# Attention logits in paired banks, one mask matmul per bank, and the last two gate projections exchanged

## The reference

```
h  = rmsnorm(x) * g
z  = h @ w_in                  # columns: QA KA VA | QI KI WI | GA | QB KB VB GB
# group A: 8 heads of 64. The indexer scores sum_h w[t,h] * relu(qi.ki) keep the top 64 keys
#          of each query (chunk-causal, chunks of 64); softmax attention over the kept keys
# group B: 4 heads, two maps each (8 maps of 64): softmax(Q1K1) - lam * softmax(Q2K2), times V,
#          headwise rmsnorm, chunk-causal mask
y  = concat(oa * silu(ga), ob * silu(gb)) @ w_out
x  = x + rmsnorm(y)
e  = (p @ w_ple_proj) * sigmoid(x @ w_ple_gate)
x  = x + rmsnorm(e)
```

## Time and profile before

| | |
|---|---|
| median of 3 runs | 405.52 us (404.76 to 406.02) |
| span of the profiled execution | 403.8 us |
| PE busy | 389.4 us, 96% |
| DVE busy | 261.8 us, 65% |
| ACT busy | 225.3 us, 56% |
| mean granted TensorE clock | 0.998 of 2.4 GHz |

### The profile page before, as it was taken

How to read it: one execution, slowest core, us unless ns; L and a number is a source line. 1 busy time by engine, 2 the same in 40 slices (tenths; PEclk the granted TensorE clock), 3 DMA queues, 4 the chain that set the end, 5 groups by cost and what they waited for, 6 DMA issues and landing times.

```text
span 403.8 us, 5700 instructions
## 1 busy us (share of the span) xinstructions
PE 389.4 (96%) x1972; PEld 315.5 (78%) x1972; DVE 261.8 (65%) x450; ACT 225.3 (56%) x451; POOL 66.3 (16%) x122
## 2 busy tenths in 40 slices
PE   7798999999999999999999999999999999999993
PEld 6696777778777888888889878677877788888882
DVE  2837686659954458668686558765995445866733
ACT  4828545665755564544684545556575556454412
POOL 1515322031500000003005411203150000000000
PEclk9999999999999999999999999999999999999999
DMA  7999626334544237467655851733464413753002
GB/s 264 310 220 348 211 58 203 106 105 138 175 117 145 73 104 241 159 211 153 196 173 164 249 152 53 209 104 104 129 185 114 148 61 107 249 146 117 0 11 93
DMA packets 32075, 61.64 MB, mean 153 GB/s; under 512 B 2384, under 2 KB 4688, under 8 KB 32048
## 3 DMA queue, kind: packets, MB, share of 16 engines
q1 hardware_dynamic: 30928, 58.01, 46.0%
q0 software_dynamic: 1120, 3.28, 4.1%
HBM read 60.23 MB, written 1.05 MB: 152 GB/s over the span
## 4 chain that ended last, share of the span: by engine, by line
PE 79%; DMA 5%; DVE 5%; ACT 3%; issue 3%; POOL 3%; SPq 1%; DVEq 0%; POOLq 0%; ACTq 0%
PE proj L926 20%; PE proj L928 19%; PE proj L927 19%; PE pv L1057 4%; PE sc L1023 3%; DMA raw<-in_w_in_dram 3%; PE sc L1030 3%; PE sc L1027 2%; PE sc L968 2%; DMA g_norm<-in_pre_norm_g_dram 2%; PE tr L1042 2%; PE sc L998 2%; DVE w_lo L682 2%; PE tr L984 1%; ACT w_hi L500 1%
## 5 line engine op out<-in xcount | busy, mean ns | idle before, releaser
L926 PE MATMUL proj<-w_hi,act_hi 128*128 128x512 f32 (+1 forms) x416 | 166.7, 401 | 1.0 <-DVE w_lo L682 0.9
L928 PE MATMUL proj<-w_hi,act_lo 128*128 128x512 f32 (+1 forms) x416 | 160.2, 385 | 0.0
L927 PE MATMUL proj<-w_lo,act_hi 128*128 128x512 f32 (+1 forms) x416 | 159.9, 384 | 0.0
L682 DVE TENSOR_TENSOR w_lo<-raw,w_hi 128x1024 fp32r<-128x1024 f32 (+1 forms) x108 | 129.0, 1211 | 19.8 <-ACT w_hi L500 18.9
L500 ACT ACTIVATE w_hi<-raw 128x1024 fp32r<-128x1024 f32 (+1 forms) x108 | 109.9, 1036 | 8.8 <-DMA raw<-in_w_in_dram 6.6
L926 PEld LDWEIGHTS proj<-w_hi,act_hi 128*128 128x128 f32 x416 | 78.5, 189 | 16.2 <-issue 1.7
L928 PEld LDWEIGHTS proj<-w_hi,act_lo 128*128 128x128 f32 x416 | 78.1, 188 | 15.8
L927 PEld LDWEIGHTS proj<-w_lo,act_hi 128*128 128x128 f32 x416 | 78.4, 188 | 12.3
L599 ACT ACTIVATE probs<-sc,neg_max 128x128 f32<-128x128 f32 (+1 forms) x64 | 26.3, 419 | 42.0 <-DVE neg_max L772 42.0
L772 DVE TENSOR_REDUCE neg_max<-sc 128x2 f32<-128x512 f32 (+1 forms) x24 | 16.6, 691 | 39.1 <-PE sc L1030 39.0
L448 POOL TENSOR_TENSOR rstd<-var,minus_half 128x1 f32<-128x1 f32 x12 | 6.7, 557 | 203.2 <-DVE var L672 188.0
(11 more groups left out here) (124 smaller groups left out, 421.0 us busy)
## 6 DMA issues: line engine op xcount, KB each, us to landing
raw<-in_w_in_dram SPq DMA_DIRECT2D x64, 512.0 KB, 3.7
raw<-in_w_out_dram SPq DMA_DIRECT2D x16, 512.0 KB, 3.3
raw<-in_w_ple_gate_dram SPq DMA_DIRECT2D x16, 512.0 KB, 4.5
raw<-in_w_in_dram SPq DMA_DIRECT2D x8, 324.0 KB, 7.4
raw<-in_w_ple_proj_dram SPq DMA_DIRECT2D x4, 512.0 KB, 3.8
resid<-in_x_dram SPq DMA_DIRECT2D x2, 512.0 KB, 7.6
g_norm<-in_post_norm_g_dram POOLq DMA_DIRECT2D x2, 512.0 KB, 5.9
g_ple<-in_ple_norm_g_dram POOLq DMA_DIRECT2D x2, 512.0 KB, 7.8
```

Source lines behind the costliest of these rows:

```text
L682: nc.vector.tensor_tensor(w_lo[:, g % SLOTS, 0:nk * cols], raw[:, g % RAW_SLOTS, 0:nk * cols], w_hi[:, g % SLOTS, 0:nk * cols].bitcast(fp3 ...
L926: nc.tensor.matmul(ps, src_hi[:, b, k0 + k, :], hi, start=(k0 + k == 0), stop=False)
L927: nc.tensor.matmul(ps, src_hi[:, b, k0 + k, :], lo, start=False, stop=False)
L928: last = nc.tensor.matmul(ps, src_lo[:, b, k0 + k, :], hi, start=False, stop=last_k)
```

## The change

Order of steps:

- The twelve S (and E) steps become six. Each does both tasks of a pair, even and odd maps, in both banks. It waits until both tasks of the pair before have had their exponentials.
- In an S step, one mask matmul per bank comes first (`start=True`) and covers all maps of the bank. The products then add onto it, issued in turn for the even map in `sc0` and the odd map in `sc1`.
- The four D steps become two, with the two halves of the array issued in turn in the same way.
- The S steps move from pieces 12, 14, 16, 18, 20, 22, 35, 36, 38, 39, 41, 43 to 12, 17, 21, 35, 40, 44. PT, PV, R, hv and hn move with them. The last PV moves from piece 46 to 52, hn for block 0 from 22 to 24, and the first PV of block 1 in group B stays at 24.
- GB now precedes GA. The output projection takes its rows 512 to 1023 (group B) first, and the transposes of `y` are split by half and spread over pieces 52, 55 and WO's 0 and 3.

The pieces themselves and the weight conversions hung on them keep their numbers.

```diff
-IN_CHUNKS = ["IDX", "QB", "KB", "VB", "QA", "KA", "VA", "GA", "GB"]
+IN_CHUNKS = ["IDX", "QB", "KB", "VB", "QA", "KA", "VA", "GB", "GA"]
...
+WO_K = [4, 6, 0, 2]
...
-    UNITS += [(_c, n, k, KU, N) for n in range(2) for k in range(0, KT, KU)]
+    UNITS += [(_c, n, k, KU, N) for n in range(2) for k in (WO_K if _c == "WO" else range(0, KT, KU))]
...
-        mms("QB", both, {3: [("TI", 0)], 5: [("D", 0)], 6: [("D", 1)]})
+        mms("QB", both, {3: [("TI", 0)], 5: [("D", 0)]})
...
-    placed = [(0, ("TI", 1)), (2, ("D", 2)), (3, ("T", "QB", 0)), (4, ("D", 3)), (5, ("T", "QB", 1)), (5, ("lam",)),
+    placed = [(0, ("TI", 1)), (3, ("D", 1)), (3, ("T", "QB", 0)), (5, ("T", "QB", 1)), (5, ("lam",)),
...
-    for n, i in enumerate([12, 14, 16, 18, 20, 22, 35, 36, 38, 39, 41, 43]):
+    for n, i in enumerate([12, 17, 21, 35, 40, 44]):
         placed += [(i, ("S", n)), (i, ("E", n))]
-    placed += [(i, ("R", n)) for n, i in enumerate([13, 15, 17, 19, 21, 23, 37, 38, 39, 40, 42, 44])]
-    placed += [(i, ("PT", n)) for n, i in enumerate([18, 22, 26, 38, 40, 42, 43, 44, 45])]
-    placed += [(i, ("PV", n)) for n, i in enumerate([19, 24, 28, 41, 42, 43, 44, 45, 46])]
-    placed += [(20, ("hv", 0)), (22, ("hn", 0)), (29, ("hv", 1)), (31, ("hn", 1))]
+    placed += [(i, ("R", n)) for n, i in enumerate([16, 16, 20, 20, 24, 24, 39, 39, 43, 43, 47, 47])]
+    placed += [(i, ("PT", n)) for n, i in enumerate([19, 22, 26, 40, 41, 45, 46, 49, 50])]
+    placed += [(i, ("PV", n)) for n, i in enumerate([20, 24, 28, 42, 43, 47, 48, 51, 52])]
+    placed += [(22, ("hv", 0)), (24, ("hn", 0)), (29, ("hv", 1)), (31, ("hn", 1))]
...
+    placed += [(52, ("t8", "y", 0, 1)), (55, ("t8", "y", 0, 0))]
...
-    for c, chunk in enumerate(["KB", "VB", "QA", "KA", "VA", "GA"]):
+    for c, chunk in enumerate(["KB", "VB", "QA", "KA", "VA", "GB"]):
         mms(chunk, both, dict(enumerate(mid[c * len(both):(c + 1) * len(both)])))
-    mms("GB", one(0), {})
-    mms("GB", one(1), {2: t8("y", 0)})
+    mms("GA", one(0) + one(1), dict(enumerate(mid[6 * len(both):])))
...
                 elif kind == "D":
...
-                    rows = slice(odd * HEAD, (odd + 1) * HEAD)
                     for j in range(2):
-                        last = nc.tensor.matmul(sc[i % 2][:, j * keys:(j + 1) * keys],
-                                                idxT[rows, j, b * P:(b + 1) * P], idxT[rows, 2, 0:keys],
-                                                start=True, stop=True)
-                    last.then_inc(dots_done, 1)
+                        for odd in range(2):
+                            rows = slice(odd * HEAD, (odd + 1) * HEAD)
+                            ins = nc.tensor.matmul(sc[odd][:, j * keys:(j + 1) * keys],
+                                                   idxT[rows, j, b * P:(b + 1) * P], idxT[rows, 2, 0:keys],
+                                                   start=True, stop=True)
+                            if j == 1:
+                                ins.then_inc(dots_done, 1)
                 elif kind == "S":
...
-                    if i < 2:
-                        pe.wait_ge(relu_done, L * 4 + 3 + i)
+                    if s[1] == 0:
+                        pe.wait_ge(relu_done, L * 4 + 4)
                     else:
-                        pe.wait_ge(exp_done, L * 12 + i - 1)
+                        pe.wait_ge(exp_done, L * 12 + 2 * s[1])
...
-                        last = nc.tensor.matmul(ps[:, first:keys], ident16[:, :], mask[:, 0:keys - first],
-                                                start=False, stop=True)
-                    last.then_inc(s_done, 1)
+
+                    for odd in range(2):
+                        nc.tensor.matmul(sc[odd][:, :].rearrange("p (m k) -> p m k", k=keys)[:, :, first:keys],
+                                         ident16[:, :],
+                                         mask[:, :].unsqueeze(1).to_broadcast([P, n_maps, keys - first]),
+                                         start=True, stop=False, skip_group_check=True)
+
+                    for j in range(n_maps):
+                        for part in range(1 if b == 0 else 3):
+                            for odd in range(2):
+                                m = s_task(2 * s[1] + odd)[2][j]
+                                rows = slice(odd * HEAD, (odd + 1) * HEAD)
...
+                                ins = nc.tensor.matmul(sc[odd][:, j * keys:(j + 1) * keys], q, k, start=False,
+                                                       stop=end, skip_group_check=True)
+                                if end and j == n_maps - 1:
+                                    ins.then_inc(s_done, 1)
```

More of the change, by code:

```diff
@@ L56 @@
     FIRST.setdefault(_u[0], _i)
+FIRST_OF = {}
+for _i, _u in enumerate(UNITS):
+    FIRST_OF.setdefault((_u[0], _u[1]), _i)
 LAST_OF = {(_u[0], _u[1]): _i for _i, _u in enumerate(UNITS)}
@@ L98, in layer_steps @@
     t8 = lambda src, b: [("t8", src, b, 0), ("t8", src, b, 1)]
+    y8 = lambda b, half: [("t8", "y", b, half)]
     if L == 0:
@@ L109, in layer_steps @@
         mms("IDX", one(1), {})
-        mms("QB", one(1), {1: [("TI", 0)], 2: [("D", 0)], 3: [("D", 1)]})
-    mid = [[] for _ in range(6 * len(both))]
-    placed = [(0, ("TI", 1)), (2, ("D", 2)), (3, ("T", "QB", 0)), (4, ("D", 3)), (5, ("T", "QB", 1)), (5, ("lam",)),
+        mms("QB", one(1), {1: [("TI", 0)], 3: [("D", 0)]})
+    mid = [[] for _ in range(7 * len(both))]
+    placed = [(0, ("TI", 1)), (3, ("D", 1)), (3, ("T", "QB", 0)), (5, ("T", "QB", 1)), (5, ("lam",)),
               (11, ("T", "KB", 0)), (13, ("T", "KB", 1)), (25, ("T", "QA", 0)), (28, ("T", "QA", 1)),
@@ L354, in t8_index @@
         def t8_index(kind, b, half):
-            return T8_BASE[kind] + 2 * b + half
+            return T8_BASE[kind] + 2 * b + (1 - half if kind == "y" else half)
         block = ctx.enter_context(nc.Block())
@@ L581, in _ @@
                 elif kind == "D":
[L582 to L586, removed]
-                elif kind == "E":
[L588 to L603, removed]
@@ new lines, in _ @@
+                    b = s[1]
+                    w = 2 * P * (b + 1)
+                    for odd in range(2):
+                        i = 2 * b + odd
+                        act.wait_ge(dots_done, L * 4 + i + 1)
+                        nc.scalar.activation(probs[:, i, 0:w], sc[odd][:, 0:w], ACT.Relu, scale=HEAD ** -0.5)\
+                            .then_inc(relu_done, 1)
+                elif kind == "E":
+                    for i in (2 * s[1], 2 * s[1] + 1):
+                        g, b, maps, keys = s_task(i)
+                        act.wait_ge(max_done, L * 12 + i + 1)
+                        if i < 4:
+                            act.wait_ge(score_done, L * 2 + i // 2 + 1)
+                        elif i - 4 in PT_OF_S:
+                            act.wait_ge(tr_done, tr_index(L, ("PT", PT_OF_S[i - 4])))
+                        else:
+                            act.wait_ge(mix_done, L * 3 + (i - 4) // 2 + 1)
+                        for j, m in enumerate(maps):
+                            last = nc.scalar.activation(probs[:, i % 4, j * keys:(j + 1) * keys],
+                                                        sc[i % 2][:, j * keys:(j + 1) * keys], ACT.Exp,
+                                                        bias=neg_max[:, i % 2, j:j + 1],
+                                                        accum_out=row_sum[:, g, b, m:m + 1])
+                        last.then_inc(exp_done, 1)
@@ L766, in _ @@
                 elif kind == "S":
[L767 to L774, removed]
+                    for i in (2 * s[1], 2 * s[1] + 1):
+                        g, b, maps, keys = s_task(i)
+                        dve.wait_ge(s_done, L * 12 + i + 1)
+                        if L * 12 + i >= 2:
+                            dve.wait_ge(exp_done, L * 12 + i - 1)
+                        nc.vector.tensor_reduce(neg_max[:, i % 2, 0:len(maps)],
+                                                sc[i % 2][:, :].rearrange("p (m k) -> p m k", k=keys), AX.X, ALU.max,
+                                                negate=True).then_inc(max_done, 1)
                 elif kind == "R":
@@ L925, in _ @@
                         last_k = u == LAST_OF[chunk, n] and k == nk - 1
-                        nc.tensor.matmul(ps, src_hi[:, b, k0 + k, :], hi, start=(k0 + k == 0), stop=False)
+                        nc.tensor.matmul(ps, src_hi[:, b, k0 + k, :], hi, start=(first_u and k == 0), stop=False)
                         nc.tensor.matmul(ps, src_hi[:, b, k0 + k, :], lo, start=False, stop=False)
@@ L967, in _ @@
                             tile = resid[:, b, k * P:(k + 1) * P]
-                        last = nc.tensor.transpose(sc[half][:, j * P:(j + 1) * P], tile, ident[:, :])
+                        last = nc.tensor.transpose(sc[i % 2][:, j * P:(j + 1) * P], tile, ident[:, :])
                     last.then_inc(t8_done, 1)
```

49 lines of the change are left out of this document (27 added, 22 removed).

## The result

The changed kernel takes 394.91 us (median of 4 runs, 394.52 to 395.67) against 405.58 us before (4 runs): ratio 0.9735, 95% interval 0.9716 to 0.9754. The forecast was 389.0 us, with 386 to 392 as its own range and 383 to 396 as the range that also held the two rivals on turns. The direction, the place of the new wait and the wider range held. The own range did not, and neither did four sizes: taking turns gave more than I took, the new wait was longer, the first PV was later than the bound that I had allowed, and a loss that I had set at nothing followed the new wait.

What follows compares the result with a forecast made beforehand. PE, busy 33.00 of 33.00 us mid-layer, was taken as the bound. Savings of 24.3 us less 6.8 for the PV wait and 1.0 allowance gave 16.5 us, hence 389.0 us, own range 386 to 392.

Steps and rivals of the forecast that it cites:

- the two rivals on turns: S and D products: turns give nothing, 393.5 us, chance 0.22; or turns give everything, 384.4 us, chance 0.13.
- What PE pays for tasks before: S tasks on PE cost 21.3 us a layer, including 128-to-64-row passages; without gain from turns, S and D save 18.8 us.
- Turns, 5.5 us: S and D products alternating between array halves take 0.08 us an instruction, not 0.107: 5.5 us more saved over both layers.
- the full gain: Both array halves work at once in S and D, 29.9 us saved on PE; as a rival 384.4 us, chance 0.13.
- The wait at PV: First PV of block 1, group B: PE waits 3.4 us a layer for hn, queued behind conversions on DVE; 6.8 us in all.
- P: Start of the piece after the third S pair (piece 22), from which the queue times up to hn were counted.
- The clock should not fall in it: During PE's 3.4 us wait before the first PV of block 1, PE keeps its full clock; no loss counted.
- The 0.5 us a layer at the first PV: Allowance for the pT copy on ACT following the second pair's exponentials; 0.5 us a layer, bounds 0 and 1.
- The exchange and the waits of S on both tasks: Swapping GA and GB with WO's row order, and S waiting for both tasks of the pair before: costed at nothing.
- the rival in which ACT and DVE hold up every pair: Each of twelve S pairs holds PE about 0.8 us beyond the sum: 398.6 us, chance 0.10.
- my first rival: Turns in S and D give nothing, products stay at 0.107 us: 393.5 us, chance 0.22.
- The slower rival: Each change between array halves in S and D costs about 0.165 us, 128 changes: 414.5 us, chance 0.05.

Runs made afterwards that it cites:

- the mask between the halves: Kernel with hv at 21 and hn at 22, each S step reordered to even mask, even products, odd mask, odd products: 389.83 us, ratio 0.9624.
- the filled one: Changed kernel plus 20 unused identity matmuls on PE ahead of the wait of the first PV of block 1: 389.89 us, ratio 0.961.
- early hn: Changed kernel with hv of block 0 at piece 21 (was 22) and hn of block 0 at 22 (was 24): 380.79 us, ratio 0.9374.

## Why the prediction came out as it did

- **What PE pays for tasks before (21.3 us a layer), one passage a pair, masks at their columns:** right. 18.8 us were to come from this without any overlap. The separate passage is a little cheaper than I had it (0.21 to 0.29 and not 0.33).
- **Turns, 5.5 us taken in the middle between 0 and 11.1:** a term mis-sized. It is the upper end. Savings on PE were 29.1 us where the full gain gave 29.9. The rows I set against it, PV at 0.105 us for 64 columns, are of matmuls that all use the same 128 rows of the array. The Trainium skill's "TensorEngine Tiling (Array Packing)", section Key Properties, says tiles load and multiply in parallel, and this case agrees: a product of each half in 0.12 us. Its other rule, that a change of mode drains the engine, agrees with the passages and with the mask between the halves.
- **The wait at PV, 3.4 us:** the mechanism was right, and for the part that I worked out the size was too (3.69 us idle with hv early). The step that failed is "In DVE's queue hn is behind the conversions": that is true, and they end 6.9 us behind P as worked out (79.04 to 85.96), but it followed only one of the two queues that hn needs. The change also moved hv past the last piece of QA in POOL's queue, and the power waited behind the rotation, 1.4 us more.
- **"The clock should not fall in it":** failed, and it is the costliest of my errors, 5.0 to 5.5 us. I took one fall after 5 us without matmuls as a sign that 3.4 us are harmless. It showed only that the clock had fallen by then: in the changed kernel it fell 3.5 and 4.4 us after the last matmul's turn. The Trainium skill's "TensorE: Matmul & The Clock Gate", section "Why this matters for your kernels", warns against idle gaps of about this size. The traces agree: all waits of 3.7 us and more in these runs lowered the clock. So did two of the idle stretches of about 2 us that each of the ten profiles has once, at the start of the kernel (last section).
- **The 0.5 us a layer at the first PV:** 1.16, above the upper bound of 1. The place was right: the wait is for the pT copy behind the second pair's exponentials.
- **The exchange and the waits of S on both tasks:** cost nothing, as said. Behind the first 35 us the changed kernel has no idle stretch of PE over 0.25 us but those at the two PVs, so the rival in which ACT and DVE hold up every pair is out.
- **How it adds up:** 16.5 us predicted, 10.7 measured: 4.8 more from PE's products and D, less 3.8 more at the wait, 1.3 at the first PV and 5.5 for the clock. So savings were set 4.8 us too low and losses 10.6 us too low. That the time still fell into the wider range is luck: the errors partly cancelled. It lies nearest to my first rival (393.5 us, turns give nothing), whose reason is wrong.
- **The slower rival:** a change between the halves was to cost some 0.165 us. Two products with the change between them take 0.12 us, about what one takes alone.

## What to carry to other kernels

In these runs two matmuls of 64 rows in different halves of the array and different banks cost about as much as one, as long as no matmul of 128 rows stands between them; exact alternation matters less than that. When a step moves in a list that several engines walk, follow each engine's queue that it passes, POOL's too, down to what a later step needs. Waits of 3.8 and 5.3 us on TensorE cost more than their length here, since work behind them ran at 1.2 GHz: move such a wait away, or else fill it.

## What the runs showed that I had not expected

- In the changed kernel the clock fell while PE still stood idle, 3.5 us after the last matmul's turn had ended (83.75 to 87.25), and came back 5.1 us after work resumed (4.4 and 6.0 us in the second layer). With the wait of 3.84 us it fell about as work resumed, and was back after 3.4 us. So the second costs less than the first by more than the difference of the waits.
- Shorter waits lower it only sometimes. At the start of the kernel PE idles for about 2 us until a first weight conversion is done. In the kernel with hv early (2.35 us idle) and in the filled one (1.90 us) the clock then fell for 3.4 us; in the kernel before (2.39 us), the changed kernel (2.24 us) and that with early hn (1.98 us) it did not. So the length of such an idle stretch does not decide it alone, and what else does is open. The row of the kernel with hv early:

```profile
13.20:16.60 3.40, 3.17 (x9) 2.49 (x10) 2.31 (x4) 1.43 (x5) 2.28 (x4) 0.50 0.96 303
```

- PE runs two groups of matmuls side by side that were issued one after the other, when they use different halves and banks, and starts one of the second group before the fourth of six of the first (70.19 against 70.30 us in the kernel without turns).
